# Expert tiles of 64 slots in both column halves of TensorE, an expert-by-expert TensorE program, and one place for the gathered rows

## The reference

```
g_idx = argmax(t @ w_rg + b_rg)                      # one of 4 groups
e_in  = (t @ w_re + b_re) of that group's 4 experts
top_v, top_i = top_k(e_in, 2)
combine = softmax(top_v) * prob(g_idx), at the two chosen experts
hid = silu(t @ w_gate[e]) * (t @ w_up[e])            # 1024 -> 256, per expert
out = sum over e of (hid * combine[e]) @ w_down[e]   # 256 -> 1024
x   = x + g2 * out
```

## Time and profile before

| | |
|---|---|
| median of 3 runs | 1652.22 us (1652.11 to 1661.51) |
| the profiled execution | 1666.19 us, its span 1664.2 us |
| mean granted TensorE clock | 0.915 |
| first gate-and-up product, last scatter's issue | 1305.09 us, 1611.51 us |
| tiles run | 26 |

### The profile page before, as it was taken

One profiled execution on the slowest core, in us unless ns is written; L12 is line 12 of the kernel. 1 busy time (PEld: TensorE's weight loads), 2 busy tenths in 40 slices (PEclk: granted clock), 3 DMA queues, 4 the chain that ended last, 5 costly groups with the idle time before them and its releaser, 6 DMA issues. The chain is left out here.

```text
span 1664.2 us, 20181 instructions
## 1 busy us (share of the span) xinstructions
PE 1409.8 (85%) x7249; PEld 811.6 (49%) x7250; DVE 776.7 (47%) x1688; ACT 448.9 (27%) x969; POOL 183.1 (11%) x377
## 2 busy tenths in 40 slices
PE   6799994994888979999968998989983699999960
PEld 1455552563653446666636666544432344444430
DVE  1411121857636768888975555323335111212117
ACT  3311111211225537666324555001110111111110
POOL 0000004002001002112110000000000223222220
PEclk9799997995878989999989999999995799999985
DMA  9300005753003142323031000543227666875828
GB/s 332 121 5 4 4 4 154 225 181 57 2 2 83 33 152 86 111 66 118 28 114 72 1 1 2 188 130 114 89 89 259 209 219 231 285 273 198 281 87 311
DMA packets 137994, 204.78 MB, mean 123 GB/s; under 512 B 27558, under 2 KB 103014, under 8 KB 137574
## 3 DMA queue, kind: packets, MB, share of 16 engines
q1 hardware_dynamic: 122642, 160.13, 29.4%
q0 software_dynamic: 10656, 32.49, 5.5%
q10 hardware_dynamic: 4612, 11.05, 1.9%
HBM read 158.71 MB, written 42.93 MB: 121 GB/s over the span
## 5 line engine op out<-in xcount | busy, mean ns | idle before, releaser
L2123 PE MATMUL ps<-ex_wgu,ex_xT 128*128 x416 | 185.1, 598 | 3.8 <-ACT ex_xT L2162 2.5
L1280 DVE TENSOR_SCALAR_CACHE_REDUCE tk_eq<-sc,tk_cand 128x512 bf16<-128x512 f32 (+4 forms) x155 | 146.8, 1007 | 0.0
L1214 PE MATMUL ps<-hT,gt_w 128*128 128x352 f32 (+1 forms) x384 | 123.9, 477 | 11.4 <-DMA gt_w<-in_w_in 11.4
L1678 PE MATMUL ps<-hT,mergedT 128*128 128x512 f32 (+1 forms) x288 | 120.3, 600 | 5.8 <-DMA op_wr<-in_w_route_expert 5.8
L2123 PEld LDWEIGHTS ps<-ex_wgu,ex_xT 128*128 128x128 f32 x416 | 77.8, 192 | 93.0 <-issue 93.0
L1214 PE MATMUL ps<-zT,gt_w 128*128 128x352 f32 (+1 forms) x384 | 120.9, 468 | 0.0
L1214 PEld LDWEIGHTS ps<-hT,gt_w 128*128 128x128 f32 x384 | 74.3, 194 | 57.4 <-DMA gt_w<-in_w_in 12.0
L2196 DVE SCALAR_TENSOR_TENSOR ex_hid<-ex_silu,ex_weight,ps 128x256 f32<-128x256 f32 x26 | 12.5, 480 | 184.9 <-ACT ex_silu L2168 184.9
L1214 PEld LDWEIGHTS ps<-zT,gt_w 128*128 128x128 f32 x384 | 73.0, 190 | 44.1
L2144 PE MATMUL ps<-ex_wd,ex_hidT 128*128 x208 | 93.6, 593 | 0.2 <-DVE ex_hidT L2203 0.2
L1243 ACT ACTIVATE mask<-sc,tk_cand 128x384 bf16<-128x384 f32 (+1 forms) x62 | 82.3, 1329 | 14.7 <-DVE tk_cand L1296 14.7
(11 more groups left out here) (462 smaller groups left out, 2106.3 us busy)
## 6 DMA issues: line engine op xcount, KB each, us to landing
ex_wgu<-in_w_gate SPq DMA_DIRECT2D x16, 1024.0 KB, 5.6
ex_wgu<-in_w_up SPq DMA_DIRECT2D x16, 1024.0 KB, 8.2
ex_wd<-in_w_down SPq DMA_DIRECT2D x16, 1024.0 KB, 5.1
sp_ada_w<-in_w_ada SPq DMA_DIRECT2D x14, 1024.0 KB
cb_y<-y_dram ACTq DMA_DIRECT2D x16, 512.0 KB, 6.9
merge_left_dram<-qiT SPq DMA_DIRECT2D x8, 544.0 KB, 6.6
mg_gb<-gate_b_dram SPq DMA_DIRECT2D x8, 544.0 KB, 3.8
mergedT<-merge_left_dram SPq DMA_DIRECT2D x8, 544.0 KB, 4.8
```

What stands on the lines that cost most here:

```text
L1214: i = nc.tensor.matmul(m.ps[:, seq % 8, 0:n], lhs, rhs[:, k, lo:lo + n], start=k == 0, stop=k == nk - 1)
L1280: return v.tensor_scalar(junk[j], m.sc[0:r, c:c + w], scalar, 0.0, op, ALU.add, accum_out=cnt[0:r, j:j + 1])
L1678: i = nc.tensor.matmul(m.ps[rows, 2 * (t % 2) + n, :], m.mergedT[:, k, t * P:t * P + r], m.wout[:, k, n * 512:(n + 1) * 512], start=k == 0 ...
L2123: j = nc.tensor.matmul(m.ps[:, 2 + b, :], xT[:, b, k, :], wgu[:, bass.ds(at, 1), k, :].rearrange("p o n -> p (o n)"), start=k == 0, stop=k ...
```

## The change

Tiles have 64 slots (`SL`), with at least two tiles for each expert; the table of slots is as much narrower and wider (64 partitions, 66 columns for each of its three fields instead of 34). In `gate_up` the stationary operand is 128 x 64, and the up columns go to the array's lower column half, the gate columns to its upper half (256 columns each); in `down` the two column blocks of 512 go to the two halves. Inputs to the transposes have 64 partitions, but the first transpose of a group keeps all 128.

TensorE's run-time tile loop becomes 16 pieces, one for each expert: a first tile, then a loop up to `expert_done`, with the weights' place fixed in each piece. `tile_place` and `tile_ready` go. The order within a tile is now `gate_up(n)`, `transposes(n+1)`, `down(n-1)`, `hidden_transposes(n)`. The other engines keep their loops over pairs of tiles.

`xg`, `xT`, `hid` and `hidT` have one place each, as has the PSUM of gate and up. The gather of tile n+1 therefore waits for `transposes(n)`. The index of the next gather is copied one tile earlier.

```diff
-MAXT = (2 * NT + NE * P) // P
+SL = 64
+MAXT = 2 * NT // SL + 2 * NE
...
-                    i = nc.tensor.matmul(m.ps[:, 2, 0:3 * MAXT], place[0:r, j, :],
+                    i = nc.tensor.matmul(m.ps[0:SL, 2, 0:3 * MAXT], place[0:r, j, :],
...
-                step(ts(tiles, exi[:, 1, :], 1.0, None, ALU.max))
+                step(ts(tiles, exi[:, 1, :], 2.0, None, ALU.max))
...
+                step(ts(m.loops[:, 2:3], m.loops[:, 0:1], 2.0, None, ALU.mult))
...
                 def gather(i, b):
                     n = 2 * i + b
-                    wait(pool, tp, 2 * n - 2)
-                    nc.gpsimd.tensor_copy(idx[:, b:b + 1], m.by_slot[:, 0, bass.ds(n, 1)]).then_inc(ic, 1)
+                    wait(pool, tp, 2 * n)
                     wait_alone(1 + b, ic, n + 1)
                     nc.gpsimd.indirect_dma_start(
-                        out=xg[:, b, :], out_offset=None, in_=m.h2_dram,
+                        out=xg[0:SL, :], out_offset=None, in_=m.h2_dram,
...
+                def transposes(n):
+                    pe.wait_ge(gl, 16 * n + 16)
                     for x in range(2):
                         for k in range(4):
+                            c, r = P * (4 * x + k), SL if x or k else P
+                            j = nc.tensor.transpose(m.ps[:, x, SL * k:SL * k + r], xg[0:r, c:c + P], m.ident[0:r, 0:r])
                         j.then_inc(tp, 1)
...
+                def gate_up(n, s):
                     pe.wait_ge(xed, n + 1)
                     pe.wait_ge(xea, n + 1)
                     for k in range(KD):
+                        for half, c in ((0, FD), (SL, 0)):
+                            j = nc.tensor.matmul(m.ps[half:half + SL, 2, 0:FD], xT[:, k, :], wgu[:, s, k, c:c + FD],
+                                                 start=k == 0, stop=k == KD - 1)
                     j.then_inc(gp, 1)
...
+                def down(n, s):
+                    pe.wait_ge(htc, n)
+                    pe.wait_ge(yea, n)
+                    pe.wait_ge(yed, n)
+                    for f in range(2):
+                        for c in range(2):
+                            j = nc.tensor.matmul(m.ps[SL * c:SL * (c + 1), 4 + c, :], hidT[:, f, :], wd[:, s, f, 512 * c:512 * (c + 1)],
                                                  start=f == 0, stop=f == 1)
                     j.then_inc(dn, 1)
...
+                def body(n, e, last):
+                    gate_up(n, e % RING)
+                    transposes(n + 1)
+                    if last is not None:
+                        down(n, last % RING)
+                    hidden_transposes(n)
...
+                for e in range(NE):
+                    pe.wait_ge(here, e + 1)
+                    body(start, e, e - 1 if e else None)
+                    end = m.expert_done[0:1, e:e + 1] if e < NE - 1 else m.loops[0:1, 2:3]
+                    end = pe.value_load(end, min_val=2 * (e + 1), max_val=MAXT)
+                    with pe.Fori(start + 1, end) as n:
+                        body(n, e, e)
+                    start = end
+                down(start, (NE - 1) % RING)
...
                 def body(i):
                     for b in range(2):
                         hidden(i, b)
+                        following(xts, i, b)
                         previous(rows, i, b)
                         hidden_copy(i, b)
-                        xts(i + 1, b)
```

More of the change, by code:

```diff
@@ L1985, in experts @@
         wgu, wd = m.wgu, m.wd
[L1986 to L1994, removed]
+        idx = sb("ex_idx", [SL, 2], I32)
+        row = sb("ex_row", [SL, 2], I32)
+        wcol = sb("ex_weight", [SL, 2])
+        xg = sb("ex_x", [P, D])
+        xT = sb("ex_xT", [P, KD, SL])
+        sl = sb("ex_silu", [SL, 2, FD])
+        hid = sb("ex_hid", [P, FD])
+        hidT = sb("ex_hidT", [P, 2, SL])
+        yo = sb("ex_y", [SL, 2, D])
         idle = sb("ex_idle", [1, 9])
-        gl, ys = ([m.sem(f"ex_{n}{i}") for i in range(2)] for n in ("x_gathered", "y_stored"))
+        flag = sb("ex_flag", [1, 2])
+        gl, ys = m.sem("ex_x_gathered"), [m.sem(f"ex_y_stored{i}") for i in range(2)]
         ic, wc, rc, tp, xed, xea, gp, slr, hr, htp, htc, dn, yea, yed, here = (m.sem("ex_" + n) for n in (
@@ L2029, in previous, with following @@
                 step(i - 1, 1)
+        def following(step, i, b):
+            if b:
+                step(i + 1, 0)
+            else:
+                step(i, 1)
         with nc.Block() as block:
@@ L2126, in gate_up, with hidden_transposes @@
                     j.then_inc(gp, 1)
-                def hidden_transposes(i, b):
-                    n = 2 * i + b
+                def hidden_transposes(n):
                     pe.wait_ge(hr, n + 1)
-                    wait(pe, htc, n)
                     for f in range(2):
-                        j = nc.tensor.transpose(m.ps[:, 6, P * f:P * (f + 1)], hid[:, b, P * f:P * (f + 1)], m.ident[:, :])
+                        r = SL if f else P
+                        j = nc.tensor.transpose(m.ps[:, 6, SL * f:SL * f + r], hid[0:r, P * f:P * (f + 1)], m.ident[0:r, 0:r])
@@ L2146, in down @@
                                                  start=f == 0, stop=f == 1)
                     j.then_inc(dn, 1)
-                def body(i):
-                    for b in range(2):
-                        gate_up(i, b)
-                        previous(down, i, b)
-                        hidden_transposes(i, b)
-                        transposes(i + 1, b)
-                run(pe, body, lambda: (transposes(0, 0), transposes(0, 1)), lambda last: down(last, 1))
+                def body(n, e, last):
[4 more added lines that the diff above has]
+                    hidden_transposes(n)
@@ new lines, in _ @@
+                pe.wait_ge(yed, 1)
+                transposes(0)
+                start = 0
+                for e in range(NE):
[6 more added lines that the diff above has]
+                    start = end
@@ L2177, in body @@
                         silu(i, b)
+                        following(xts, i, b)
                         previous(rows, i, b)
-                        xts(i + 1, b)
-                run(act, body, lambda: (xts(0, 0), xts(0, 1)), lambda last: rows(last, 1))
+                nc.scalar.copy(flag[:, 0:1], m.ones[0:1, 0:1]).then_inc(yea, 1)
+                run(act, body, lambda: xts(0, 0), lambda last: rows(last, 1))
             @block.vector
@@ L2212, in body @@
                         hidden(i, b)
+                        following(xts, i, b)
                         previous(rows, i, b)
                         hidden_copy(i, b)
-                        xts(i + 1, b)
-                run(dve, body, lambda: (xts(0, 0), xts(0, 1)), lambda last: rows(last, 1))
+                v.memset(xg[SL:P, 0:P], 0.0)
+                v.memset(hid[SL:P, 0:P], 0.0)
+                v.tensor_copy(flag[:, 1:2], m.ones[0:1, 0:1]).then_inc(yed, 1)
+                run(dve, body, lambda: xts(0, 0), lambda last: rows(last, 1))
 def combine(nc, m, O):
```

109 lines of the change are left out of this document (37 added, 72 removed).

## The result

The changed kernel takes 1734.49 us (median of 4 runs, 1731.81 to 1741.43), the kernel before, run with it, 1653.95 (4 runs, 1652.11 to 1661.51). The ratio is 1.0484, with a 95% interval from 1.0437 to 1.0532: slower by 80.5 us. The forecast was 1665 us, in a range from 1640 to 1706.

What follows compares the result with a forecast made beforehand. TensorE was taken to set the pace: 46 tiles of 6.70 us, 308 against 296. Ends +6.6, shorter last scatter -0.5, late gathers +6.5 give +12.6 on the median 1652.2: 1665 us, range 1640 to 1706 for 8 in 10.

Steps and rivals of the forecast that it cites:

- The tile: Experts' loop on TensorE: 5.86 us of work plus 0.84 for six changes of form, 6.70 us a tile, 46 tiles.
- the reason that was named: Column halves in the experts' loop: padding falls by 11.5%, from 3328 slots to 2944, while a slot costs 18% more.
- the price: TensorE, each change of form between groups: 0.14 us lost, six times a tile, 0.84 us.
- The other engines: Experts' loop: VectorE's work, 2.6 us of a 6.7 us tile, lies behind TensorE; register loads are free.
- the table: Table of slots ahead of the experts: its 36 records take 12 us against 8.8; the table is ready 4.8 us later.
- both ends: Start and tail of the experts' loop: first product at about 1305.4 as before, last scatter +6.6 us and 0.5 shorter.
- The gather: Fetch of a tile's rows into one place: 4.6 us ordinarily, hidden; 5.9 us behind a weight load, with 5.4 available.
- 13 x 0.5 = 6.5 us: Gathers behind the 13 weight loads issued in the loop: each 0.5 us too late, 6.5 us in all.
- The upper bound, 13 x 2.8: Gathers with 128-row times: 2.8 us for each of the 13, about 0.3 for each of the rest, 46 us.
- the gather decides: Rival on the gathers: 64 rows take as long as 128, with idle time ahead of every transposes group; 1704 us, 15%.
- A fall of the clock: Rival on TensorE: the clock falls in the shorter groups; placed near 1900 us, 2%.
- the short waits of 4 us: Experts' loop before: three short waits after one-tile experts, 4 us of the 306, go with two tiles for each expert.

Runs made afterwards that it cites:

- f1: Against e1: all transposes take 64 rows and small products take the waits, 4 changes of form a tile instead of 6; 1659.32 us, ratio to before 0.9999.
- e1: Against the changed kernel: gathers go into two places, one tile further ahead, and ScalarE copies each to where TensorE reads; 1677.96 us, ratio to before 1.0123.
- e3: Against the changed kernel: eight thrown-away products between gate-and-up and transposes in the first tile of experts 1 to 13; 1714.27 us, ratio to before 1.0331.
- f5: Against f4: two gathers may be in flight, each place with its own count of landings; 1644.87 us, ratio to before 0.9917.
- e2: Against the changed kernel: SyncE issues an expert's gate and up load only when the next gather has landed; 1725.98 us.
- f2: Against f1: `down` right behind gate-and-up and both transpose groups together, 2 changes of form a tile; 1657.59 us, ratio to before 0.9990.
- f4: Against f2: first two transposed pieces copied by themselves, waits ahead of transposes held by plain semaphore instructions on TensorE's queue; 1653.04 us, ratio to before 0.9973.

## Why the prediction was wrong

**The tile.** Forecast 6.70 us, measured 6.77; gate-and-up starts every 6.77 us, each group 0.07 us ahead of the end of the one before it at a change of form, and 46 tiles ran. So the halves do give TensorE almost nothing here, for the reason that was named; f1 fits the price, 0.27 us for two changes and what went with them (no run changes the number of changes alone). 46 x 0.07 = 3 us more than in the sum.

**The other engines, the table and both ends.** VectorE ends no idle time of TensorE but 0.7 us ahead of the last `down`. From the last gate-and-up to the last scatter's issue it took 10.7 us (1664.80 to 1675.49), forecast 10.5. The first product was to start as before; leaving out the 12 us of the earlier stage, it starts about 2 us earlier. The table's 36 records took 8.6 us, where 12 were forecast, for the clock was up in part of them.

**The gather: the step that failed.** Its place, its count and its cause were right: 13 waits, each behind a weight load, none elsewhere. The term "13 x 0.5 = 6.5 us" was mis-sized: 39.3 us, 3.0 a wait. The larger part is the landing: the forecast put the gather of 64 rows behind a load at 5.9 us, because half the bytes would take less. It took 7.3 to 8.7, in the mean 8.1, as long as 128 rows did. The long gathers of before were long for the load ahead of them and not for their own bytes, and that part does not halve; the ordinary ones did get shorter (3.6 to 4.1 us, forecast 4.6). The smaller part, 0.3 us a wait, is GpSimd's chain ahead of the DMA: 0.8 us instead of 0.45, mostly because "issue" took 0.46 us where the earlier trace rows have 0.15, so 5.1 us were left and not 5.4. The upper bound, 13 x 2.8, was close. Of the rivals "the gather decides" came nearest, but its short waits ahead of all other tiles did not come. The rows that tell it were there: the long gathers in the earlier trace rows lay 2.4 us above the median, and the load of the earlier trace rows had been issued 1.85 us ahead of one of them.

**The clock: the step that was missing.** The sum had no term for what an idle stretch does to the work behind it. A fall of the clock was given 2%, and looked for in the shorter groups; it came after the waits and cost 28 us. That is why the rival in which the gather decides, at 1704 us, was still 30 too low.

With the measured terms the sum is 12.6 - 6.5 + 39.3 + 28.2 + 3.2 = 76.8 us, against 78.3 in the stage and 80.5 in the medians. That 67.5 us of it hang on the late gathers is shown by e1, which takes them out of the stage; that 28 of these are the clock's, by e3. What is left of e1 over before, 10.8 us in the stage, is the tile (46 x 6.77 against 26 x 11.40 us is 15 more), less the short waits of 4 us that the prediction had go. The single profiled executions leave some 8 us open between the stage's lengths and the medians (e1 18.5 against 10.8, f5 11.9 against 20.3); no run here settles where they are. The stages ahead, which are the same in all kernels but for the table, reach the first product anywhere from 1290.8 to 1305.1 us in the eleven profiled executions.

## What to carry to other kernels

A transfer that was issued just behind a big load was late here by the load, not by its own size: the transfer was halved and the delay stayed, and 1.2 us more between load and transfer (e2) hardly helped. So keep the lead, or a second place, when a change cuts the work that hid it. An idle stretch on TensorE is to be priced twice here, once for the wait and once for the slower products behind it (39 and 28 us); filling it with products that are thrown away, as in e3, paid 20 us although they do nothing. With column halves, group the work by form before counting on them (6.77 us a tile with six changes, 6.09 with two and the waits moved), and keep a wait out of the middle of a pair.

## What was not expected of the hardware

- Of 12 of the 13 gathers issued 1.2 to 1.6 us after a 2 MB load no packet ran for 4.4 to 4.6 us; with no load ahead, the first packet came after 1.6 us. The time between held 1.0 to 1.1 MB of the load, and as much with 2.8 us between load and gather (e2).
- The granted clock fell from 1.0 to 0.5 after each of the 13 idle stretches of 2.2 to 3.6 us, and stayed there for 3.4 to 6.8 us, in which TensorE worked. With products in the same stretches it stayed at 1.0 (e3).
- Plain semaphore instructions on TensorE's queue held the waits without stopping the products ahead of them: with them and the earlier copy the tile fell from 6.36 to 6.09 us (f2, f4). How the 0.27 us divide between the two was not measured.
